# A hybrid decoder layer with a mixture of experts: two-choice dispatch tables, twelve item widths, and a reordered attention loop

## The reference, cut to what matters

```python
def one_block(args):                      # attention, one block of 128 queries
    logits = einsum('bqhd,bkhd->bhqk', q_blk, k) * scale + (c_q[..., :, None] - c_k[:, :, None, :])
    p = softmax(where(causal, logits, -inf), axis=-1)
    return einsum('bhqk,bkhd->bqhd', p, v)
...
mix = concatenate([_rmsnorm(rec, ...), _rmsnorm(att, ...)], axis=-1)
x = x + mix @ w_out
...
def _moe(h, ...):
    logits = xt @ w_router + b_router
    top_vals, top_idx = lax.top_k(logits, 4)
    gates = softmax(top_vals)
    ...                                   # tokens sorted by expert
    gu = x_blk @ w_gate_up[e] + b_gate_up[e]
    g = minimum(gu[:, :1024], 7.0); u = clip(gu[:, 1024:], -7.0, 7.0)
    act = (u + 1.0) * (g * sigmoid(1.702 * g))
    y = (act @ w_down[e] + b_down[e]) * gate        # added up per token
```

## Time and profile before

| | |
|---|---|
| median of 3 runs | 2010.98 us (2010.34 to 2013.39) |
| profiled execution, its own time | 2016.19 us |
| span of the profiled execution | 2014.4 us |
| TensorE busy | 1896.6 us (94%) |
| VectorE busy | 1276.9 us (63%) |
| ScalarE busy | 1050.2 us (52%) |
| GpSimd busy | 399.2 us (20%) |
| HBM | 255 GB/s over the span |

### The profile page before, as it was taken

One profiled execution on the slowest core, in us unless ns is written; L12 is line 12 of the kernel. 1 busy time (PEld: TensorE's weight loads), 2 busy tenths in 40 slices (PEclk: granted clock), 3 DMA queues, 4 the chain that ended last, 5 costly groups with the idle time before them and its releaser, 6 DMA issues.

```text
span 2014.4 us, 51108 instructions
## 1 busy us (share of the span) xinstructions
PE 1896.6 (94%) x20629; PEld 1755.8 (87%) x20629; DVE 1276.9 (63%) x2642; ACT 1050.2 (52%) x1442; POOL 399.2 (20%) x302
## 2 busy tenths in 40 slices
PE   6999988989967999999999999999999999999895
PEld 4777756658857999999999999999999999999895
DVE  4553636765377555556666666567767767767865
ACT  5575425543114445455555555566656656656554
POOL 4000000001002111112111122222333333333423
PEclk9999989999978999999999999999999999999998
DMA  4111010005457777788888889998999999999992
GB/s 143 43 52 42 21 63 1 2 1 181 157 197 260 239 268 271 270 274 286 294 297 294 295 286 326 323 324 287 356 349 364 351 359 368 352 356 365 355 364 71
DMA packets 251385, 478.76 MB, mean 238 GB/s; under 512 B 17312, under 2 KB 38096, under 8 KB 251264
## 3 DMA queue, kind: packets, MB, share of 16 engines
q1 hardware_dynamic: 231040, 443.59, 61.1%
q0 software_dynamic: 20256, 33.94, 7.6%
HBM read 466.96 MB, written 47.19 MB: 255 GB/s over the span
## 4 chain that ended last, share of the span: by engine, by line
PE 55%; DVE 7%; issue 5%; ACT 2%; DVEq 0%; POOL 0%; ACTq 0%; POOLq 0%
PE E_p_d L1943 23%; PE E_p_g L1932 5%; PE E_p_g L1935 5%; PE E_p_g L1934 5%; PE E_p_u L1932 5%; PE E_p_u L1935 5%; PE E_p_u L1934 5%; DVE E_w_lo L1773 4%; PE E_p_t L1914 2%; PE E_p_t L1899 2%; ACT E_w_hi L1687 1%; DVE E_up L1833 1%; DVE E_gate L1821 1%; DVE E_gate L1827 1%; DVE E_peak L1767 0%
## 5 line engine op out<-in xcount | busy, mean ns | idle before, releaser
L1773 DVE SCALAR_TENSOR_TENSOR E_w_lo<-E_w_st,E_w_hi 128x2048 f16<-128x2048 f32 x260 | 594.7, 2287 | 60.3 <-ACT E_w_hi L1687 56.6
L1687 ACT ACTIVATE E_w_hi<-E_w_st 128x2048 f16<-128x2048 f32 x260 | 492.6, 1905 | 143.6 <-PE E_p_g L1935 96.7
L1943 PE MATMUL E_p_d<-E_a_f,E_w_st 128*128 128x160 f32 (+6 forms) x4096 | 531.0, 288 | 16.8 <-DVE E_a_f L1843 16.8
L1943 PEld LDWEIGHTS E_p_d<-E_a_f,E_w_st 128*128 128x128 f32 x4096 | 515.2, 191 | 25.0 <-issue 14.9
L1932 PE MATMUL E_p_g<-E_x_hi,E_w_hi 128*128 128x160 f16 (+6 forms) x2048 | 372.9, 224 | 8.3 <-issue 8.3
L1932 PE MATMUL E_p_u<-E_x_hi,E_w_hi 128*128 128x160 f16 (+6 forms) x2048 | 371.7, 223 | 5.0 <-DVE E_w_lo L1773 5.0
L1934 PE MATMUL E_p_g<-E_x_lo,E_w_hi 128*128 128x160 f16 (+6 forms) x2048 | 372.9, 224 | 0.0
L1935 PE MATMUL E_p_g<-E_x_hi,E_w_lo 128*128 128x160 f16 (+6 forms) x2048 | 372.9, 224 | 0.0
L1935 PE MATMUL E_p_u<-E_x_hi,E_w_lo 128*128 128x160 f16 (+6 forms) x2048 | 371.6, 223 | 0.0
L1934 PE MATMUL E_p_u<-E_x_lo,E_w_hi 128*128 128x160 f16 (+6 forms) x2048 | 371.6, 223 | 0.0
L1631 POOL DMA_INDIRECT out<-E_y_rows,E_idx_out x66 | 168.4, 2552 | 590.6 <-ACT E_y_rows L1705 566.0
(11 more groups left out here) (375 smaller groups left out, 2761.0 us busy)
## 6 DMA issues: line engine op xcount, KB each, us to landing
E_w_st<-in_w_gate_up SPq DMA_DIRECT2D x130, 2048.0 KB, 10.0
E_w_st<-in_w_down SPq DMA_DIRECT2D x64, 2048.0 KB, 14.6
A_w_st<-in_w_in SPq DMA_DIRECT2D x20, 512.0 KB, 3.9
A_x_rows<-in_x SPq DMA_DIRECT2D x8, 512.0 KB, 8.8
C_x_res<-in_x SPq DMA_DIRECT2D x8, 512.0 KB, 4.5
x_rows<-C_x SPq DMA_DIRECT2D x8, 512.0 KB, 5.0
out<-C_x SPq DMA_DIRECT2D x8, 512.0 KB, 5.8
h_rows<-C_h SPq DMA_DIRECT2D x8, 512.0 KB, 4.5
```

The costliest lines, as they stand in the source:

```text
L1687: act.activation(w_hi[c % RI][:], staged(c % NG), ACT.Copy, scale=SW).then_inc(hi_s, 1)
L1773: dve.scalar_tensor_tensor(out=w_lo[c % RI][:], in0=staged(c % NG), scalar=SW, in1=w_hi[c % RI][:], op0=ALU.mult, op1=ALU.subtract, accum_ ...
L1943: ins = pe.matmul(banks[:, h, 0:w], staged(c)[:, k, h * P:(h + 1) * P], x[:, k, 0:w], start=h == 0 and k == 0, stop=k == KT - 1, skip_grou ...
```

## The change

`WIDTHS` gets four more classes (184, 168, 152, 136) and class limits go in steps of 8. In stage B each probability tile is scaled with its inverse row sum before it is transposed (`normal`, on ScalarE for three tiles and on VectorE for one); the transposed tiles of the early block go to `p_o[1]`, those of the late block to `p_t`; `weigh(u, 0)` comes last in the loop; the mean squares are kept as one column per block, and inverted once at the end. In stage C the square root is taken of that column form, between ScalarE's second and third copy, and TensorE spreads it over the partitions; idle products are added around the last block. In stage D the tables are f16 with pairs of choice columns innermost, gates go as a high and a low half, and 28 idle products stand before the first row product. In stage E the first two borders are read ahead, one branch leaves both classes out, and four idle products follow the first transpositions.

```diff
-WIDTHS = (256, 192, 176, 160, 144, 128, 112, 96)
+WIDTHS = (256, 192, 184, 176, 168, 160, 152, 144, 136, 128, 112, 96)
+GROUP = 2
+FINE = 8
...
+        def home_of(n):
+            return p_o[1] if n % 4 >= 2 else p_t
...
             def weigh(u, side):
...
-                pe.wait_ge(inv_s, u + 1)
...
-                for e in range(2):
-                    pe.matmul(p_o[0][e * HD:(e + 1) * HD, o + P:o + 2 * P],
-                              row_inv[:, n + e:n + e + 1].to_broadcast([P, HD]), m.ident[:], start=True, stop=True)
...
+                turn(n + 2)
                 turn(n + 1)
                 if u + 1 < NU:
                     score_pair(n + 6)
-                turn(n + 2)
-                weigh(u, 0)
                 turn(n + 3)
                 if u % 4 == 1 and u > 4:
                     sums(u // 4 - 1)
+                weigh(u, 0)
...
+            def normal(n):
+                L = P * (where(n)[0] + 1)
+                act.wait_ge(inv_s, 2 * (n // 4) + 1 + n % 4 // 2)
+                act.activation(tile_of(n)[:, 0:L], tile_of(n)[:, 0:L], ACT.Copy, scale=row_inv[:, n:n + 1]
+                               ).then_inc(norm_act, 1)
...
+            def normal(n):
+                L = P * (where(n)[0] + 1)
+                dve.wait_ge(inv_s, 2 * (n // 4) + 1)
+                dve.tensor_scalar(tile_of(n)[:, 0:L], tile_of(n)[:, 0:L], row_inv[:, n:n + 1], None,
+                                  ALU.mult).then_inc(norm_dve, 1)
...
-                dve.tensor_tensor(m.att[:, u % 4, rows_of(u // 4, side)], m.att[:, u % 4, rows_of(u // 4, side)],
-                                  p_o[0][:, o + P:o + 2 * P], ALU.mult).then_inc(out_s, 1)
+                dve.tensor_copy(m.att[:, u % 4, rows_of(u // 4, side)], p_o[0][:, o:o + P]).then_inc(out_s, 1)
...
-                for side in range(2):
-                    step(dve.reciprocal(m.att_ms[:, rows_of(q, side)], m.att_ms[:, rows_of(q, side)]))
...
             for g in range(CT):
                 act.activation(mix_hi[:, g, :], m.rec[:, g, :], ACT.Copy).then_inc(mix_hi_s, 1)
-            act.activation(att_rs[:], m.att_ms[:], ACT.Sqrt).then_inc(att_ok, 1)
+                if g == 1:
+                    act.activation(att_rs[:], m.att_ms[:], ACT.Sqrt).then_inc(att_ok, 1)
...
             rec_part(0)
+            pe.wait_ge(att_ok, 1)
+            for t in range(T):
+                ins = pe.matmul(p_m[t // 4][:, t % 4 * P:(t % 4 + 1) * P], att_rs[:, t:t + 1].to_broadcast([P, P]), m.ident[:],
+                                start=True, stop=True)
+                if t % 4 == 3:
+                    ins.then_inc(rs_mm, 1)
...
             route(T - 2)
+            pe.wait_ge(x2_s, T - 1)
+            keep_warm(3)
             turn(T - 1)
+            keep_warm(5)
             route(T - 1)
...
-                dve.tensor_tensor(one_lo[:, w, :], m.iota_lo[:].unsqueeze(1).to_broadcast([P, GROUP, P]),
-                                  lo_f[:, w].unsqueeze(2).to_broadcast([P, GROUP, P]), ALU.is_equal)
-                for q in range(GROUP * g, GROUP * (g + 1)):
-                    dve.tensor_scalar(val_row[:, q, :], m.iota_hi[:], hi_f[:, q:q + 1], m.row_no[:, q:q + 1],
-                                      ALU.is_equal, ALU.mult).then_inc(row_s, 1)
+            for g in range(0, NG, BATCH):
+                at_g = slice(g, g + BATCH)
+                step(dve.tensor_tensor(one_hi[:, at_g], each(m.iota_hi, SLOTB), spread(hi_f[:], SLOTB), ALU.is_equal))
+                dve.tensor_tensor(one_lo[:, at_g], each(m.iota_lo, P), spread(lo_f[:], P), ALU.is_equal)
+                dve.tensor_tensor(val_row[:, at_g], one_hi[:, at_g], spread(m.row_no[:], SLOTB), ALU.mult).then_inc(row_s, 1)
...
+                dve.tensor_tensor(val_gate[:, at_g, 0], one_hi[:, at_g], spread(ex_hi[:], SLOTB), ALU.mult)
+                dve.tensor_tensor(val_gate[:, at_g, 1], one_hi[:, at_g], spread(ex_lo[:], SLOTB), ALU.mult).then_inc(gate_s, 1)
...
+            for _ in range(28):
+                pe.matmul(p_warm[:], m.ident_b[:], m.ident_b[:].unsqueeze(1).to_broadcast([P, 4, P]), start=True, stop=True)
...
+            with eng.If(early[-1] > 0):
+                lo = 0
+                for v in range(EARLY):
+                    one_class(lo, early[v], WIDTHS[v])
+                    lo = early[v]
+                eng.nop()
+            lo = early[-1]
+            for v in range(EARLY, NV):
+                hi = border(eng, v)
+                one_class(lo, hi, WIDTHS[v])
                 lo = hi
...
             n_items = count(pe)
+            early = early_borders(pe)
```

207 lines of the change are left out of this document (131 added, 76 removed).

## The result

The changed kernel takes 1980.70 us (median of four runs, 1979.4 to 1987.1), beside 2010.66 us for the kernel before on the same chip: a ratio of 0.9855 with a 95% interval of 0.9831 to 0.9878 (taken over all runs; the two medians alone give 0.9851), faster by 30.0 us. The forecast was 49.5 us and 1961.5 us; the measured median lies at the very end of its range, 1981. The sign is right; the size is not. The profiled execution took 1982.0 us with a span of 1980.2, so the two spans differ by 34.2 us, where the working said 49.5.

The account below looks back on a forecast made before the run. TensorE was taken to bound wide expert items and be busiest in attention. Gains of 17.0 (widths), 4.1 (expert start), 5.9 (dispatch) and 24.3 (attention), less 1.8 (output stage), gave 49.5 us: median 1961.5 us, range 1954 to 1981.

Parts of the forecast that it names:

- Attention: Attention stage: 16.8 us from loops, 2.85 from reciprocals in three loops, 4.6 at its end; 24.3 us gained in all.
- The walk: Attention: one 8.79 us loop followed through the new order to 7.45 us; 1.2 us a loop taken over 14 loops.
- the sign that the prediction had named: Attention: loops waiting for scaled tiles would show the prediction wrong; no size given.
- rival 2: Attention: scaling of probability tiles binds, loops keep their length, 16.8 us less gain, 1978.3 us; chance 0.17.
- The tail: End of attention: two reciprocals, two multiplications and the last loop's serial transpose, copy and weighting go; 4.6 us gained.
- The start of the expert stage: Expert stage: first transpositions to first expert product falls to 8.4 us, VectorE's own limit; 4.1 us gained.
- Dispatch: Dispatch stage: faster 16-bit tables and earlier gather put first transpositions at 34.9 us against 40.9; 5.9 us gained.
- rival 1: Dispatch: 16-bit tables run at the f32 rate, 7.7 us less gain, 1969.2 us; chance 0.12.
- Width classes: Expert stage: eight items lose 8 columns, 2.12 us each; 17.0 us gained, lower bound 15.5 if 136-column items wait.
- Class entries: Expert stage: ten entries with items in place of six, costed at nothing because TensorE's queue covers border read and branch.
- Rival 3: Expert stage: each class entry stalls TensorE for code, ten costing 83 us, 2044 us in all; chance 0.03.
- Output stage: Output stage: 3.9 us lost at its start, 1.8 gained at its end by keeping the clock; net 1.8 us lost.

Follow-up runs that it names:

- copies last: Changed kernel with the six output-weight copies moved out of the attention loops to behind them; 1984.06 us (one run).
- reciprocals first: Changed kernel with the short side's reciprocals issued ahead of the low part of an output weight on VectorE; 1980.99 us, ratio 0.9831.
- together: Changed kernel with reciprocals before weight copies, root and spreading first in output stage, four weight loads later, border reads between transposition groups; 1973.78 us, ratio 0.9801.
- no pair: Changed kernel with the two choices outside the columns of the 16-bit dispatch tables, not innermost; 1982.54 us (one run).
- attention as before: Changed kernel with the old kernel's attention stage and start of the output stage; 1991.56 us, ratio 0.9895.

## Why the prediction was wrong in size

**Attention, the step that failed most** ("I walked one loop of 8.79 us ... I take 1.2 us a loop over 14 loops"): 16.8 and 2.85 us for the loops, 10.0 measured. The walk left work out. The walked loop was not an empty one; ScalarE's high part of an output weight lies just ahead of it, VectorE's low part in it, and ScalarE's squares at its end:

```profile
335.89 1.04 ACT L916 ACTIVATE wo_hi<-B_wo_raw 128x1024 fp32r<-128x1024 f32 x1
...
344.79 1.13 ACT L892 ACTIVATE B_square<-att 128x512 f32<-128x512 f32 x2
...
337.47 1.21 DVE L1001 TENSOR_TENSOR wo_lo<-B_wo_raw,wo_hi 128x1024 fp32r<-128x1024 f32 x1
```

They are not in its 5.9 us of ScalarE and 6.3 us of VectorE: in the changed kernel's loop at 353.15 us, of the same width and without them, both engines are busy for 5.9 us, and it takes 7.51 us. In the changed kernel this very loop takes 8.72 us, where the walk said 7.45; with copies last it takes 7.73. For loops without copies, squares or sums the walk was good: 8.4 to 8.6 us in the first width (8.4 forecast), 7.5 in the second, 7.2 in the third (7.0 forecast). The fourth has no such loop; with copies last one takes 7.15. Multiplying by 14 then gave all loops the gain of these. Five of the six loops with a weight copy lose by it. Before, the transpositions did not wait for the reciprocals; after, they do, and so hang on the copies through one chain: VectorE waits for the high part, makes the low part, and only then the reciprocals; ScalarE waits 1.37 us for these before it scales, and in three loops TensorE waits 0.43 to 1.73 us for scaled tiles, the sign that the prediction had named. Copies last shows 6 us for the copies, reciprocals first 2.6 of these for one bad place in VectorE's order. With the copies on GpSimd the stretch of all loops takes 123.98 us, 17.4 less than the 141.35 before; 19.65 was forecast. ScalarE's share of the whole stage, which I used against rival 2, could not show such a chain. Rival 2 was half right: scaling binds loops with other work (7.7 us for the stage in all), not the clean ones. The tail was right (5.0 us, 4.6 forecast). The stage's start gained 1.2 that I had not counted, and that is luck: from the stage's start to the first wide score group the same code takes 2.3 us in some traces and 3.3 to 3.5 in others.

**The start of the expert stage** ("I take 8.4 us, which is VectorE's own limit, a gain of 4.1 us"): 1.3 measured. VectorE's limit is 8.7 us, as three traces with a short jump show. The failed part is that the jump was left out of the sum as covered. It waits for code, and the code waits behind weight loads: 6.1 to 6.6 us with them in flight, 3.6 to 3.9 without. Before, TensorE waited twice (3.5 and 4.1 us, a 16 KB packet of the instruction queue in each) with the DMA engines about half busy; the change took one wait away, and the one left grew to 6.4. The Trainium skill (Runtime: NRT & Kernel Launch, Instruction fetch mechanics) says that a taken branch out of the fetched pages stalls for a DMA fetch, and the traces agree; that the weight traffic adds some 2.5 us is shown by this case's traces.

**Dispatch** ("So the gather sets the first transpositions: 34.9"): 36.7 measured. Tables, row rate and row numbers came out as forecast, and rival 1 is out. The rule of the Trainium skill (Vector Engine (DVE) Microarchitecture Reference, section 5.1) held in both directions: 0.57 us with the innermost pair, 0.97 without. What failed is that I let the border reads run beside the gather. All engines leave the dispatch stage together and GpSimd leaves only when its gather has landed, so two reads (1.3 us) come behind it; that they move as a whole, together shows. The larger miss was not of a stage but of its worth: no pair shows that of the 5.1 us which the pair takes out of dispatch 2.5 are gone at the first product, because the jump then meets the weight traffic. At the second item 1.5 us are left by the changed kernel's own trace, 2.1 to 3.4 by four others; that difference is mostly the clock in the first item.

**Width classes** (17.0): 14.1. The lower bound had the mechanism, other engines making TensorE wait at 136 columns, but 1.4 us each was too much (0.76 and 0.95), and the first item gained 1.7, not 2.1. Class entries cost nothing, as forecast: at each of them the first product follows the last transposition as inside a class. Rival 3 is out.

**Output stage** (-1.8): -2.9. The start was right (3.4 lost, 3.9 forecast). At the end "1.8 gained" became 0.3 in this trace: the clock had fallen ahead of the last transpositions in spite of the idle products, which then took 2.1 us themselves. That is bad luck more than a wrong step. In the trace of attention as before, which has the old start and the new end, the stage takes 118.2 us in place of 120.0, about the 1.8 gained. In six of nine traces with the changed stage it takes 121.5, 1.5 lost. Without the idle products it is 1.2 us worse than here, 2.6 worse than there.

**The base.** "5.2 us over the median ... and the median 1961.5": the profiled execution of before lay 5 us above its median, that of after 1.3 us. Such offsets don't carry over. With the budget's 15.3 us this makes up the 19.2 us between forecast and median.

What stays open: how the clock's phase falls, in attention (153.8 or 158.3 us for the same code) and at the output stage's end (121.5 or 122.6 to 124.1), and whether one order of expert 0's loads can serve gather, jump and first item at once; three orders were tried.

## What to carry to other kernels

Walk every kind of loop, each with all that its engines do in it, and multiply by kind; a small copy that nobody waited for can stand in a chain once the order changes. Before crediting an earlier start, ask what is in flight at the new moment: here weight loads, gathered rows and the code of a taken branch share the DMA engines, so of 5 us won in one stage half was gone at the next one's first product. An idle engine that is slow at the work (GpSimd, twice VectorE's time) can be the best place for work that nobody waits for; ask first which of the other engine's operations it will hold up.

## Unexpected about the hardware

- A taken branch on TensorE lasts 3.6 to 3.9 us with the DMA engines nearly empty and 6.1 to 6.6 us with them full of weight loads, and over one class body as long as over two (6.27 and 6.39). The packet with the code takes 0.9 to 1.1 us either way; it starts 0.9, 1.5 or 3.8 us behind the branch.
- A gather of 128 rows lands 4.9 us after its issue without weight loads beside it and 7.8 us among them.
- A scaling of 1024 columns on VectorE, from SBUF to SBUF, takes 0.75 us alone and up to 2.36 us when GpSimd is in a subtraction, and then ends 0.56 us behind it.
- Idle products are no sure hold on the clock: three of them straight ahead of the last eight transpositions of the output stage kept these on the full clock in nine traces (1.09 us) and not in five (1.91 to 1.97 us). The five ahead of the router product held it in all fourteen (1.87 to 1.97 us; 3.62 without).
